# Three gate and up tiles per operand tile at a feed-forward's entry, with panels fetched early and the first block's work reordered

## The reference, cut to what matters

```python
D_MODEL, SEQ, D_FF, FFN_RES = 1024, 1024, 2816, 0.5

def _rmsnorm(x, g):
    xf = x.astype(jnp.float32)
    y = xf * lax.rsqrt(jnp.mean(xf * xf, axis=-1, keepdims=True) + EPS)
    return (y * g.astype(jnp.float32)).astype(x.dtype)

def _swiglu(h, w_gu, w_down):
    g, u = jnp.split(h @ w_gu, 2, axis=-1)
    return (jax.nn.silu(g) * u) @ w_down

    x = x + FFN_RES * _swiglu(_rmsnorm(x, norm_ffn1[l]), w_ffn1_gu[l], w_ffn1_down[l])
...
    x = x + FFN_RES * _swiglu(_rmsnorm(x, norm_ffn2[l]), w_ffn2_gu[l], w_ffn2_down[l])
```

## Time and profile before

| | us |
|---|---|
| three runs | 3335.28, 3343.84, 3335.58 |
| their median | 3335.58 |
| the profiled execution, its own time | 3338.5 |
| span of that execution in the trace | 3336.4 |
| mean granted clock of PE, share of full speed | 0.993 |

### The profile page before, as it was taken

The page is one execution under the profiler, slowest core; times in us unless marked ns, Lnnn a source line. Parts: engine busy times, 40 slices in busy tenths (PEclk is TensorE's granted clock), DMA queues, the critical chain, the costliest instruction groups (busy, mean ns, idle before and its releaser), DMA issues.

```text
span 3336.4 us, 47997 instructions
## 1 busy us (share of the span) xinstructions
PE 3248.6 (97%) x19068; PEld 1655.5 (50%) x19068; DVE 1818.1 (54%) x2813; ACT 1131.2 (34%) x2104; POOL 1803.1 (54%) x1352
## 2 busy tenths in 40 slices
PE   8999998999999799999999999999999999999999
PEld 4555653655565344444445545555545444444444
DVE  4365558236545887775113376665666687676100
ACT  1434422233341523231002455555555342323000
POOL 4555752446675277674333465555665438777332
PEclk9999999999999999999999999999999999999999
DMA  3112112112021211112222111111112121111312
GB/s 133 41 49 62 59 61 90 53 40 77 26 89 39 82 56 58 64 51 98 71 67 93 32 53 53 56 48 52 36 53 90 47 101 53 62 64 38 109 52 79
DMA packets 59275, 211.70 MB, mean 63 GB/s; under 512 B 7344, under 2 KB 7728, under 8 KB 58544
## 3 DMA queue, kind: packets, MB, share of 16 engines
q1 hardware_dynamic: 54304, 191.34, 17.6%
q10 hardware_dynamic: 4752, 17.30, 1.3%
HBM read 181.36 MB, written 20.97 MB: 61 GB/s over the span
## 4 chain that ended last, share of the span: by engine, by line
PE 94%; DVE 3%; issue 1%; ACT 1%; POOL 1%; DMA 0%; DVEq 0%; POOLq 0%; ACTq 0%
PE pair L1184 27%; PE pair L1185 26%; PE pair L1186 26%; PE pair L1404 3%; PE pair L1373 3%; PE pair L1385 2%; PE pair L1622 1%; PE pair L1648 1%; PE pair L1633 1%; PE pair L1576 1%; PE pair L1204 1%; DVE arena L2155 1%; PE pair L1362 0%; POOL panel_parts L967 0%; ACT residual L1905 0%
## 5 line engine op out<-in xcount | busy, mean ns | idle before, releaser
L1184 PE MATMUL pair<-operand,panel_parts 128*128 128x512 f16 x1808 | 693.2, 383 | 47.8 <-DVE operand L2155 26.1
L966 POOL TENSOR_SCALAR panel_parts<-panel_raw 128x1024 f16<-128x1024 f32 (+3 forms) x204 | 209.0, 1024 | 920.7 <-issue 654.4
L1185 PE MATMUL pair<-operand,panel_parts 128*128 128x512 bf16 x1808 | 690.6, 382 | 0.0
L1186 PE MATMUL pair<-operand,panel_parts 128*128 128x512 f16 x1808 | 690.4, 382 | 0.0
L1184 PE MATMUL pair<-arena,panel_parts 128*128 128x512 f16 (+1 forms) x1248 | 471.3, 378 | 8.9 <-issue 4.4
L967 POOL TENSOR_TENSOR panel_parts<-panel_raw,panel_parts 128x1024 bf16<-128x1024 f32 (+3 forms) x204 | 469.2, 2300 | 17.0
L1003 POOL TENSOR_SCALAR arena<-arena,row_inv 128x256 f32<-128x256 f32 (+7 forms) x256 | 344.6, 1358 | 236.4 <-DVE row_inv L2221 236.1
L1185 PE MATMUL pair<-arena,panel_parts 128*128 128x512 bf16 (+1 forms) x1248 | 470.5, 377 | 0.0
L1186 PE MATMUL pair<-arena,panel_parts 128*128 128x512 f16 (+1 forms) x1248 | 470.3, 377 | 0.0
L1184 PEld LDWEIGHTS pair<-operand,panel_parts 128*128 128x128 f16 x1808 | 177.5, 98 | 283.1 <-issue 94.8
L2158 DVE SCALAR_TENSOR_TENSOR residual<-pair,residual 128x1024 f32<-128x1024 f32 (+1 forms) x64 | 61.3, 958 | 420.0 <-PE pair L1186 392.1
(11 more groups left out here) (300 smaller groups left out, 5979.1 us busy)
## 6 DMA issues: line engine op xcount, KB each, us to landing
panel_raw<-in_wl SPq DMA_DIRECT2D x58, 512.0 KB, 3.5
panel_raw<-in_wm SPq DMA_DIRECT2D x56, 512.0 KB, 3.6
ffn_extra<-in_wgu SPq DMA_DIRECT2D x18, 1024.0 KB, 5.0
panel_raw<-in_wgu SPq DMA_DIRECT2D x18, 1024.0 KB, 5.1
panel_raw<-in_wdn SPq DMA_DIRECT2D x32, 512.0 KB, 3.5
residual<-residual_spill SPq DMA_DIRECT2D x31, 512.0 KB, 6.9
residual_spill<-residual ACTq DMA_DIRECT2D x24, 512.0 KB, 2.6
panel_raw<-in_wgu SPq DMA_DIRECT2D x16, 512.0 KB, 3.6
```

What stands on the lines that cost most here:

```text
L966: chained(nc.gpsimd.tensor_scalar(hi[:, c], RAW[:, s, c], HI_MAX, -HI_MAX, ALU.min, ALU.max))
L1184: nc.tensor.matmul(out, stat[0], mov[0], start=first, stop=False, skip_group_check=skip)
L1185: nc.tensor.matmul(out, stat[0], mov[1], start=False, stop=False, skip_group_check=skip)
L1186: return nc.tensor.matmul(out, stat[1], mov[0], start=False, stop=last, skip_group_check=skip)
```

## The change

It has five parts.

1. At the first feed-forward, PE runs tiles (0,0), (0,1) and (0,2) for each operand tile, 18 matmuls, and the sum of squares follows directly. At the second it keeps two, and tile (0,2) follows as before.
2. The first two panels of each feed-forward are fetched early by one load of 1 MB into `EXR` (`early_panels`): in the second layer behind its last residual loads, and at the third turn of the mixer. POOL splits them into `EARLY`, at the same place in its order as before, and panels (0,2) and (0,3) behind them with no wait for a tile. The squares of x get other buffers (`SQT`), so that `EXR` is free.
3. The first block's raw weights are loaded behind the first panels, after the early panels are split. DVE makes the first block's weight sums ahead of `plain_pair(1)`, ACT starts its first weight copy behind silu 0.
4. T4 is brought forward: ACT copies it, and POOL makes its remainder, ahead of the block's last two weight parts.
5. In the first block DVE runs `evict(0, 0)` between the two halves of `plain_pair(3)`, and `evict(0, 1)` and `evict(0, 2)` ahead of the second block's weight sums.

```diff
@@ -334,8 +334,8 @@
                  ("rms2", 1, (3,)), ("gu2", PLAIN_F // 2, 4), ("down2", 2, 4)]
-PANEL_SECTIONS = [("layers", 1, len(LPANELS)), ("gu1", PLAIN_F // 2, 4), ("down1", 2, 12),
-                  ("mix", 1, len(MIX_PANELS)), ("out", 1, 1), ("gu2", PLAIN_F // 2, 4), ("down2", 2, 12)]
+PANEL_SECTIONS = [("layers", 1, len(LPANELS)), ("gu1a", 1, 2), ("gu1", PLAIN_F // 2 - 1, 4), ("down1", 2, 12),
+                  ("mix", 1, len(MIX_PANELS)), ("out", 1, 1), ("gu2a", 1, 2), ("gu2", PLAIN_F // 2 - 1, 4), ("down2", 2, 12)]
@@ -374,6 +374,11 @@
+def gu_panel(idx, i, j):
...
+    return (f"gu{idx}a", 0, j - 2) if i == 0 else (f"gu{idx}", i - 1, j)
@@ -464,7 +469,7 @@
         EXR = EX[:, 0:2048]
-        SQT = [arena(c, 1024) for c in (11264, 12288, 26624, 27648, 22528, 24576)] + [EXR[:, 0:1024], EXR[:, 1024:2048]]
+        SQT = [arena(8192 + 1024 * k, 1024) for k in range(KT)]
@@ -477,6 +482,9 @@
+        def slot_parts_of(v):
+            return v.bitcast(HI)[:, 0:1024], v.bitcast(LO)[:, 1024:2048]
@@ -491,7 +499,7 @@
         HOME = {"av0": parts(12288, 1024), "mq0": parts(5120, 1024)}
-        THIRD_FFN = {1: parts(18432, 1024), 2: parts(17280, 1024)}
+        EARLY = [slot_parts_of(EX[:, 2048 + 1024 * n:3072 + 1024 * n]) for n in range(2)]
@@ -781,6 +791,9 @@
+            def early_panels(idx):
+                sp.dma_start(EXR.rearrange("p (j c) -> p j c", j=2), io[f"wgu{idx}"][0, 0:2].rearrange("j p c -> p j c")).then_inc(early_loaded, 16)
@@ -861,25 +874,31 @@
                 residual_back(l, (2, 3, 6, 7))
+                if l == LAYERS - 1:
+                    early_panels(1)
...
             def ffn(idx):
-                for i in range(PLAIN_F // 2):
-                    for j in range(4):
-                        panel(f"gu{idx}", i, j, io[f"wgu{idx}"][i, j])
-                for b in range(BLOCKS):
+                def raw(b):
                     f = PLAIN_F + b
-                    if b == 0:
-                        sp.wait_ge(square_added, 7 * idx)
-                    elif b == 1:
-                        for j in (2, 3):
-                            sp.wait_ge(panel_split[panel_slot(f"gu{idx}", j)], panels_before(f"gu{idx}", PLAIN_F // 2 - 1, j) + 2)
-                    else:
-                        sp.wait_ge(weight_lo, 7 * block_of(idx, b - 1))
...
+                for i in range(PLAIN_F // 2):
+                    for j in range(2 if i == 0 else 0, 4):
+                        panel(*gu_panel(idx, i, j), io[f"wgu{idx}"][i, j])
+                    if i == 0:
+                        sp.wait_ge(early_split, 2 * idx)
+                        raw(0)
+                for b in range(1, BLOCKS):
+                    if b == 1:
+                        for j in (2, 3):
+                            sp.wait_ge(panel_split[panel_slot(f"gu{idx}", j)], panels_before(f"gu{idx}", PLAIN_F // 2 - 2, j) + 2)
+                    else:
+                        sp.wait_ge(weight_lo, 7 * block_of(idx, b - 1))
+                    raw(b)
@@ -915,6 +934,8 @@
                     sp.wait_ge(mix_max, 2 * TT * j)
+                if j == 2:
+                    early_panels(2)
@@ -1046,18 +1067,21 @@
                 restart()
-                for j in range(2):
-                    panel(f"gu{idx}", 0, j, 1024, None)
-                panel(f"gu{idx}", 0, 2, 1024, (gate_r_made, 2 * MIX_TURNS) if idx == 2 else None, THIRD_FFN[idx])
-                panel(f"gu{idx}", 0, 3, 1024, tile_done(f"gu{idx}", 0, 1))
+                pool.wait_ge(early_loaded, 16 * idx)
+                for n in range(2):
+                    raw, (hi, lo) = EXR[:, 1024 * n:1024 * (n + 1)], EARLY[n]
+                    chained(nc.gpsimd.tensor_scalar(hi, raw, HI_MAX, -HI_MAX, ALU.min, ALU.max))
+                    nc.gpsimd.tensor_tensor(lo, raw, hi, ALU.subtract).then_inc(early_split, 1)
+                for j in (2, 3):
+                    panel(*gu_panel(idx, 0, j), 1024, None)
...
                         else:
-                            used = turn_before(f"gu{idx}", i, j + 2)
-                        panel(f"gu{idx}", i, j, 1024, used)
+                            used = tile_done(f"gu{idx}", 0, j + 2) if i == 1 else turn_before(f"gu{idx}", i, j + 2)
+                        panel(*gu_panel(idx, i, j), 1024, used)
@@ -1073,9 +1097,11 @@
                 term_rest(B_T2, Q22, 0)
-                for i in range(7):
+                for i in range(5):
...
                 term_rest(B_T4, Q21, 1)
+                for i in range(5, 7):
+                    weight_rest(0, i)
@@ -1476,29 +1502,36 @@
             def ffn(idx, xbase, before=None):
-                def gu(i, j, home=None):
+                def gu_weights(i, j):
+                    if i == 0 and j < 2:
+                        pe.wait_ge(early_split, 2 * (idx - 1) + j + 1)
+                        return EARLY[j]
+                    return weights(*gu_panel(idx, i, j))
...
+                def gu(i, j):
                     dst = acquire(f"gu{idx}", i, j)
-                    w = weights(f"gu{idx}", i, j)
-                    w = home or w
+                    w = gu_weights(i, j)
...
-                dsts = [acquire(f"gu{idx}", 0, j) for j in range(2)]
-                ws = [weights(f"gu{idx}", 0, j) for j in range(2)]
+                first = 3 if idx == 1 else 2
+                dsts = [acquire(f"gu{idx}", 0, j) for j in range(first)]
+                ws = [gu_weights(0, j) for j in range(first)]
...
                     pe.wait_ge(x_split, xbase + k + 1)
-                    for j in range(2):
+                    for j in range(first):
...
                             m.then_inc(tile_ready[j], 1)
-                gu(0, 2, THIRD_FFN[idx])
+                if first == 2:
+                    gu(0, 2)
@@ -1939,6 +1972,9 @@
                         act.wait_ge(term_ready, 2 * idx)
+                    elif b == 0 and i < 4:
+                        j = i // 2
+                        act.wait_ge(tile_ready[j], tiles_before(f"gu{idx}", 0, j) + 1)
@@ -1959,17 +1995,18 @@
                 plain_silu(0)
+                weight_part(0, 0)
...
                 plain_silu(1)
-                for i in range(5):
+                for i in range(1, 5):
...
                     plain_silu(f)
+                act.wait_ge(tile_ready[3], tiles_before(f"gu{idx}", PLAIN_F // 2, 3))
+                term_part(B_T4, Q21, 12)
...
                     weight_part(0, i)
-                act.wait_ge(tile_ready[3], tiles_before(f"gu{idx}", PLAIN_F // 2, 3))
-                term_part(B_T4, Q21, 12)
@@ -2566,12 +2603,19 @@
                 def plain_pair(f):
+                    plain_front(f)
+                    plain_back(f)
...
+                def plain_front(f):
...
+                def plain_back(f):
+                    i, j = divmod(f, 2)
@@ -2651,25 +2695,32 @@
                 term_sum(Q21, Q21, Q22, 12, 11)
-                plain_pair(1)
...
                     weight_sum(0, n)
+                plain_pair(1)
...
                 term_split(B_T3, Q12, 2)
-                plain_pair(3)
+                plain_front(3)
                 term_clip(B_T4, 4).then_inc(term_clipped, 1)
+                evict(0, 0)
+                plain_back(3)
...
                         keep_block(b - 1)
-                    evict(b, 0)
+                    if b > 0:
+                        evict(b, 0)
+                    else:
+                        evict(b, 1)
+                        evict(b, 2)
...
                             weight_sum(b + 1, n)
-                    evict(b, 1)
-                    evict(b, 2)
+                    if b > 0:
+                        evict(b, 1)
+                        evict(b, 2)
```

2 lines of the change are left out of this document (added).

## The result

The changed kernel takes 3345.67 us (median of 17 runs, 3343.45 to 3347.01), the kernel before, timed in the same 17 rounds, 3339.49 (3335.28 to 3343.95). The ratio is 1.0014, with an interval of 1.0007 to 1.002: 4.7 us slower by the ratio, 6.2 by the medians, within 0.3%. The forecast was +6.2. The execution that was profiled, 3347.01, is the longest of the 17, so the profiles differ by more than the medians.

The account below looks back on a forecast made before the run. PE, busy 97% of the span, was taken as the bound, leaving 88 us idle plus low clock. Terms +0.4 + 0.7 + 2.9 + 2.2 = +6.2 on a median of 3335.58 gave about 3342, range 3324 to 3350.

Parts of the forecast that it names:

- (b): First block: T2's remainder on POOL begins ahead of DVE's T1 subtraction instead of behind it, making DVE 3.9 us later.
- for the weight sums: First block: sums now ahead of plain_pair(1) meet POOL's split of panel (1,2), making DVE 3.0 us later.
- the low clock hides in the next wait: First blocks: low clock behind new waits costs nothing, as PE ends at the next wait; else 1.4 to 2.7 us.
- The discount of 2.5: First two blocks: new waits of 11.0 us taken as 8.5, as the old order's count came out 2.5 too long.
- the walk: First two blocks: step-by-step count of engine turns, giving new waits of 3.4 + 3.1 + 1.7 + 2.8 = 11.0 us.
- the first block's lag: Second block takes over part of the first's delay, waiting 1.7 us at its fourth and 2.8 at its sixth product.
- First entry: First feed-forward's entry: three PE waits gone, -1.4 us, against 1.8 lost beside POOL's split of panel (0,3); net +0.4.
- the term for the panel: First feed-forward's entry: POOL's split of panel (0,3) beside DVE's chain costs 1.8 us, bounds 0 and 3.2.
- the 1.4: First feed-forward's entry: with 18 matmuls per operand tile, PE's three waits between tiles go, -1.4 us.
- Second entry: Second feed-forward's entry: the 3.28 wait stays; POOL's split of panel (0,3) delays DVE's operand tile, +0.7 us, bounds 0 and 2.1.
- The early fetch as such: Second entry: fetching panels earlier changes nothing, since POOL's split stays behind the mixer's last piece; the 3.28 us wait remains.
- Later blocks: Blocks behind the first ones stay at 18.35 us in the first feed-forward and 18.13 in the second.

Follow-up runs that it names:

- part 5 alone: The kernel before with only the change's reordered first-block evictions and split plain_pair(3): 3338.04 us, ratio 0.9987 to the kernel before.

## Why the prediction was right, point by point

The differences of the two profiled executions come from start times, those above, those of the earlier trace rows, and the second block's sixth product in both stages and the second stage's fourth, of the kernel before:

```profile
1256.61 0.38 PE L1184 MATMUL pair<-operand,residual 128*128 128x512 f16 x1
...
2778.64 0.38 PE L1184 MATMUL pair<-arena,ffn_extra 128*128 128x512 f16 x1 [0.30 <-DVE residual L2155]
...
2808.46 0.38 PE L1184 MATMUL pair<-operand,residual 128*128 128x512 f16 x1
```

So the first stage's second block stands 1260.53 - 1256.61 = 3.92 later, the second's 2813.58 - 2808.46 = 5.12, and each row below is the difference to the stretch ahead of it:

| stretch | forecast | measured |
|---|---|---|
| before the first entry | 0 | +1.8 |
| first entry, to tile (0,3) | +0.4 | -1.0 |
| first feed-forward, first blocks | +2.9 | +3.2 |
| its later blocks, down projection and mixer | 0 | -1.4 |
| second entry | +0.7 | +0.3 |
| second feed-forward, first blocks | +2.2 | +2.2 |
| its later blocks and the rest | 0 | +3.4 |
| sum | +6.2 | +8.5 |

*The first block: right, step by step.* T2's remainder got ahead of T1's subtraction, as (b) said. T3's subtraction was put at 1224.2 and ended at 1224.28, `evict(0, 2)` was put at 1239.0 and ended at 1238.69; since tile (0,3) itself came 0.7 later, both were 0.6 to 1.0 earlier than forecast. Counted from tile (0,3), T3's subtraction was 6.2 late, where 6.9 was forecast, and the experiments divide that much as forecast: 3.7 for the order of T1 and T2, where 3.9 was taken, 2.5 for the weight sums, where 3.0 was, and nothing left with the sums put back. The split into waits was off: 2.52, 1.12, 0.87 and 2.37, 6.9 in sum, where 3.4, 3.1 (1239.0 less 1236.0 is 3.0), 1.7 and 2.8 were walked and 8.5 taken. The low clock made up for it: 4.27 for 12 matmuls, 1.7 lost, between the fourth and the sixth product, so that PE arrived late at its sixth and waited less. That the low clock hides in the next wait was right. The discount of 2.5 had no better reason than that the walk was too long once; that 6.9 + 1.7 came to it is luck.

The Trainium skill (SBUF — State Buffer, section "SBUF: two separate sides") says that of a VectorE step with two SBUF inputs and a GpSimd instruction that reads SBUF the one that starts first has their common port pair for its whole length, and the other is fully blocked. T1's subtraction agrees: 0.56 behind T2's remainder it ended 2.15 after that remainder's end, and 2.29 is its length where it goes first.

*What the second block's waits are: wrong in its reason.* The prediction had the second block take over the first block's lag. With the lag gone (sums put back) the waits stayed, with part 5 alone a 2.37 came too, and with the new order in every block they went. They come from the order of evictions and weight sums in the block where it changes back.

*First entry: wrong in sign, the term for the panel right.* DVE's chain was late by 1.9 (1.8 forecast), and holding the panel back took 2.5 off. What PE gained was more than the 1.4: from the first operand tile to tile (0,3) it took 35.95 instead of 38.89. Of these 2.9, some 1.9 is the three waits, because a row's idle time is less than what is lost (last section), and some 1.0 is low clock, which lasted about five matmuls less. With the tiles undone, and with the panel held back, the time did not change measurably, so these parts of the entry are worth next to nothing, which is what was forecast.

*Second entry.* The POOL wait of 3.28 stayed (3.19). The operand tiles waited 0.87 and 0.45, where 0.7 was taken; that PE stayed at full clock behind the 3.19, where it had taken 5.58 for 20 matmuls behind the 3.28, 1.3 too much, took most of it back. The early fetch as such gave nothing, as forecast.

*Later blocks: the step that failed.* The prediction read 18.35 and 18.13 as properties of the two stages and left the second as it was. The second profile of the kernel before has 18.35 in both. So the +3.4 in the table need not be the change's cost: the kernel before pays it in some executions. How often each kernel does, two profiles of one and one of the other do not say; the changed kernel's runs lie closer together (3343.45 to 3347.01, against 3335.28 to 3343.95), so it may pay it every time.

*The stretches with nothing new but an early load.* They differ as much without it. PE's last matmul ahead of the first entry's wait ends between 1114.49 and 1118.44 in the four profiles of kernels without the load (1115.75 before, 1117.50 in the changed kernel). From the first feed-forward's last first copy to PE's start behind the POOL wait of the second entry, the four take 1133.0 to 1134.7 (1134.7 before, 1133.2 in the changed kernel). So the +1.8 and -1.4 lie within the scatter, and no row shows a cost of the early loads.

*The sum.* Without these two stretches and the later blocks it is -1.0 + 3.2 + 0.3 + 2.2 = +4.7. That this is the ratio's 4.7, and that the medians differ by the forecast's 6.2, is in part luck: the low clock at the entries comes and goes, and the forecast was off in opposite directions at the first entry (+0.4 for -1.0) and in the later blocks (0 for +3.4). The forecast time of 3342 lies 3.7 below the measured 3345.67, because the three runs it starts from, 3335.58, were 3.9 below the median of 17.

What the runs did not settle: why a stage takes one period or the other. In the profile with the sums put back, one program had both, and only in the second stage did PE fall to the low clock behind the second block's last wait; with the evictions back behind the sums both stages did, and both took the fast one. In the kernel before, the fast one came behind 13 matmuls at the low clock and the slow one behind 8. The other profiles fit this. Eight kernels keep the old order in the later blocks and were profiled, which makes 16 stages. In six the last long wait is in the first block: three with 23.76 to 24.30 between their first and second first copy are slow, three with 24.78 to 25.29 fast. In ten it is in the second block: seven with 19.86 to 21.70 between the second and third first copy are slow, three with 22.52 to 23.38 fast. That a PE held back longer lets DVE and POOL catch up is a guess from this; it was not tried by itself.

## What to carry to other kernels

Where two engines hold each other up, as VectorE's and GpSimd's long steps do here (6.04 instead of 2.29 for one subtraction), an operation moved forward in one engine's order changes who comes first at several later places; walk the turns, with the long operations first, before counting a wait as gone. When a hand-written order is changed for the first block alone, look at the block where it changes back: here that step cost a wait of 2 to 3 us in each stage, and the same order in every block cost nothing. A short wait that returns in every block can weigh as much as a long one at the start: 0.22 in 15 blocks is 3.3 us a stage, where the long one was 3.65, and moving one eviction ahead of one subtraction gave 7 us.

## What was not expected of the hardware

A wait shown as 0.06 costs 0.22. A matmul's row is 0.38 long but the next starts 0.216 after it, so the idle time of a row leaves out 0.16 of each wait: the 0.52 of the earlier trace rows is a fourth product that comes 0.68 late, and the blocks at 18.35, which take 0.22 more than those at 18.13, show PE busy for 18.29, so 0.06 idle.

The low clock need not cost anything. The fourth product's wait of 2.52 was followed by 12 matmuls in 4.27 instead of 2.59, and the wait behind it was shorter by that: 1.12, where the profile with the panel held back, at full clock behind the same 2.52, has 2.81, and the sixth product starts 8.15 behind the fourth in both. With the evictions back behind the sums the clock fell behind waits of 6.27 and 7.96 (first rows 0.58 and 0.59 long), and both stages ran their later blocks at 18.13, where the changed kernel, with the same order in these blocks, took 18.35.
